# The second product of an MLP by Strassen's seven block products, with its sums on GpSimd

## The reference, cut to what matters

```python
D_MODEL, SEQ, D_FF = 1024, 512, 4 * 1024

def second_block(x, ...):
    ...
    h = rms_norm_2(x, norm_mlp[l])
    x = x + jnp.square(jax.nn.relu(h @ w_up[l])) @ w_down[l]
    return rms_norm_2(x, norm_final)
```

## Time and profile before

| | before |
|---|---|
| median of 3 runs | 1278.03 us (1277.8 to 1279.31) |
| the profiled execution: time | 1278.07 us |
| the profiled execution: span of the core | 1276.3 us |
| PE busy | 1226.8 us of the span (96%) |
| DVE, ACT, POOL busy | 669.9, 554.9, 119.0 us |
| mean granted TensorE clock | 0.989 of full speed |

### The profile page before, as it was taken

One profiled execution on the slowest core, in us unless ns is written; L12 is line 12 of the kernel. 1 busy time (PEld: TensorE's weight loads), 2 busy tenths in 40 slices (PEclk: granted clock), 3 DMA queues, 4 the chain that ended last, 5 costly groups with the idle time before them and its releaser, 6 DMA issues.

```text
span 1276.3 us, 16512 instructions
## 1 busy us (share of the span) xinstructions
PE 1226.8 (96%) x6162; PEld 1018.2 (80%) x6162; DVE 669.9 (52%) x1039; ACT 554.9 (43%) x952; POOL 119.0 (9%) x193
## 2 busy tenths in 40 slices
PE   7999999989999989999989899989999999999996
PEld 5877887768888788887778798877898888888885
DVE  5556567855333365683476665445553343443443
ACT  4456686674233245533665454342342241331321
POOL 2023223200000011000132000010000000000000
PEclk9999999999999999999999999999999999999998
DMA  5321233112333533342120455311323233323221
GB/s 169 99 67 50 69 87 110 34 51 68 98 99 108 188 117 117 83 140 76 33 108 25 149 140 172 118 50 40 94 87 111 84 99 99 99 99 99 84 97 66
DMA packets 148226, 120.64 MB, mean 95 GB/s; under 512 B 4865, under 2 KB 123713, under 8 KB 148162
## 3 DMA queue, kind: packets, MB, share of 16 engines
q1 hardware_dynamic: 142672, 106.05, 28.1%
q10 hardware_dynamic: 5490, 13.73, 3.1%
HBM read 115.55 MB, written 4.22 MB: 94 GB/s over the span
## 4 chain that ended last, share of the span: by engine, by line
PE 87%; DVE 6%; ACT 3%; DMA 2%; issue 1%; POOL 0%; ACTq 0%; DVEq 0%; SPq 0%
PE lin L748 26%; PE lin L750 25%; PE lin L749 25%; PE tr L906 2%; DVE w_lo L1877 2%; DMA x_m<-in_x 1%; PE sc L916 1%; PE sc L918 1%; PE tr L899 1%; ACT w_hi L1257 1%; PE lin L942 1%; DVE neg_max L1902 1%; DMA w_raw<-in_w_xkv 1%; PE lin L941 1%; DVE h_lo L1872 1%
## 5 line engine op out<-in xcount | busy, mean ns | idle before, releaser
L1877 DVE TENSOR_TENSOR w_lo<-w_raw,w_hi 128x1024 fp32r<-128x1024 f32 x194 | 237.5, 1229 | 236.7 <-ACT w_hi L1257 226.2
L748 PE MATMUL lin<-h_hi,w_hi 128*128 128x512 f32 (+1 forms) x848 | 326.2, 385 | 5.0 <-DVE h_lo L1872 4.6
L750 PE MATMUL lin<-h_hi,w_lo 128*128 128x512 f32 (+1 forms) x848 | 318.2, 375 | 0.0
L749 PE MATMUL lin<-h_lo,w_hi 128*128 128x512 f32 (+1 forms) x848 | 317.9, 375 | 0.0
L1257 ACT ACTIVATE w_hi<-w_raw 128x1024 fp32r<-128x1024 f32 x194 | 204.0, 1055 | 240.2 <-PE lin L750 164.9
L748 PEld LDWEIGHTS lin<-h_hi,w_hi 128*128 128x128 f32 x848 | 160.9, 190 | 34.2 <-DVE h_lo L1872 5.3
L750 PEld LDWEIGHTS lin<-h_hi,w_lo 128*128 128x128 f32 x848 | 160.6, 189 | 29.0
L749 PEld LDWEIGHTS lin<-h_lo,w_hi 128*128 128x128 f32 x848 | 161.1, 190 | 25.3 <-issue 0.2
L748 PE MATMUL lin<-w_hi,u_hi 128*128 128x512 f32 x256 | 99.6, 389 | 0.0
L749 PE MATMUL lin<-w_lo,u_hi 128*128 128x512 f32 x256 | 99.6, 389 | 0.0
L750 PE MATMUL lin<-w_hi,u_lo 128*128 128x512 f32 x256 | 99.6, 389 | 0.0
(11 more groups left out here) (318 smaller groups left out, 1915.6 us busy)
## 6 DMA issues: line engine op xcount, KB each, us to landing
w_raw<-in_w_in SPq DMA_DIRECT2D x74, 512.0 KB, 3.9
w_raw<-in_w_up SPq DMA_DIRECT2D x32, 512.0 KB, 4.0
w_raw<-in_w_down SPq DMA_DIRECT2D x32, 512.0 KB, 3.6
w_raw<-in_w_out SPq DMA_DIRECT2D x16, 512.0 KB, 3.6
w_raw<-in_w_xkv SPq DMA_DIRECT2D x16, 512.0 KB, 4.3
w_raw<-in_w_branch SPq DMA_DIRECT2D x8, 512.0 KB, 3.8
w_raw<-in_w_xq SPq DMA_DIRECT2D x8, 512.0 KB, 3.7
w_raw<-in_w_xo SPq DMA_DIRECT2D x8, 512.0 KB, 3.7
```

The lines of the kernel that those rows point to most:

```text
L748: pe.matmul(o, lh, rh, start=start, stop=False)
L749: pe.matmul(o, lh, rl, start=False, stop=False)
L750: return pe.matmul(o, ll, rh, start=False, stop=stop)
L1877: return dve.tensor_tensor(out, x, as_f32(hi), ALU.subtract)
```

## The change

The chunk's down product is taken as a product of 2 x 2 blocks: u has blocks of 256 tokens x 512 hidden, `w_down`'s chunk blocks of 512 hidden x 512 columns. Instead of the 8 block products there are 7 (`DOWN`), each of 2 token tiles x 4 x 3 = 24 matmuls, on sums and differences of blocks.

- **Weights**: the four blocks of `w_down` are loaded into eight buffers `wd_a`, `wd_b` of 128 x 1024. POOL forms four sums or differences of them, each in two parts, in place (`weights_sum`, 8 instructions of 128 x 1024). ACT and DVE split the seven operands, 14 halves, into the same four slots (`down_hi`, `down_lo`).
- **Tokens**: u is kept unsplit in `u_raw`; POOL forms four sums of its blocks (`u_sum`, 4 instructions of 128 x 1024), and ACT and DVE split these too (`u_sum_hi`, `u_sum_lo`).
- **Results**: the seven products lie in the PSUM banks `sc`, `tr` and `lin`. ACT copies the first to `u2`; DVE adds products from PSUM to `x_res`, `u2` and `u3` (`add_down`, 14 instructions of 128 x 512 in place of 8), and POOL adds `u2` and `u3` to `x_res` (`add_partial`, 4 instructions of 128 x 1024).
- **Written out**: the chunks are no loop on any engine. SP's loads of `w_down` stand between those of `w_up`.
- **The end**: the square sums are taken in halves of a row, and the tiles are stored in the order 2, 3, 0, 1 (`FINAL_ORDER`).

```diff
+A11, A12, A22, S1, S2, S3, S4 = range(7)
+B11, B12, B21, B22 = range(4)
+DOWN = [Product("z", A11, 4, B11), Product("q", S3, 7, B12), Product("r", A12, 9, B21), Product("z", S2, 10, B11),
+        Product("v", A22, 9, B21), Product("z", S1, 11, B11), Product("q", S4, 12, B22)]
...
 @block.gpsimd
+            for it in range(FF_CHUNKS):
...
+                weights_sum(it, 0, B12, B22, B12, ALU.subtract)
+                pool.wait_ge(u_lo_s, UP_SPLITS * it + 4)
+                u_sum(it, 0, (0, 0), (0, 0), (1, 0), ALU.subtract)
+                split_done(pool, down_half(it, 0, 1))
+                weights_sum(it, 1, B11, B12, B11, ALU.add)
+                pool.wait_ge(u_lo_s, UP_SPLITS * it + 9)
+                u_sum(it, 1, (1, 0), (1, 0), (1, 1), ALU.add)
+                u_sum(it, 2, (1, 1), (1, 1), (0, 0), ALU.subtract)
+                pool.wait_ge(m1_copied, 2 * it + 2)
+                add_partial(it, 0, 0, 0, "u2")
+                split_done(pool, down_half(it, 2, 1))
+                weights_sum(it, 2, B21, B21, B11, ALU.subtract)
+                u_sum(it, 3, (0, 1), (0, 1), (1, 1), ALU.subtract)
+                split_done(pool, down_half(it, 3, 1))
+                weights_sum(it, 3, B11, B22, B11, ALU.subtract)
+                pool.wait_ge(down_read, 14 * it + 6)
+                add_partial(it, 1, 1, 0, "u3")
+                add_partial(it, 2, 1, 1, "u3")
+                pool.wait_ge(down_read, 14 * it + 12)
+                add_partial(it, 3, 0, 1, "u2")
...
 @block.tensor
+                for n, product in enumerate(DOWN):
+                    pe.wait_ge(u_lo_s, UP_SPLITS * it + product.splits)
...
+                    elif n == 5:
+                        pe.wait_ge(down_read, 14 * it + 4)
...
+                        for part in range(2):
+                            split_done(pe, down_half(it, n, part))
+                            for tile in range(2):
+                                mm = part_of_tile(part, tile)
...
 @block.vector
-                    for t in range(NT):
-                        add_to_x(G["mlp"][8 + 4 * j + t], t, j, off)
...
+                for k in range(OPS):
+                    if k == 5:
+                        dve.wait_ge(x_added, 4 * it + 1)
+                        add_down(it, 2, of_x(0, 0), of_x(0, 0))
+                    elif k == 7:
+                        add_down(it, 3, partial("u2"), partial("u2"))
+                        add_down(it, 1, partial("u3"), partial("u2"), 3)
+                    elif k == 9:
+                        dve.wait_ge(x_added, 4 * it + 2)
+                        add_down(it, 4, of_x(1, 0), of_x(1, 0))
+                    elif k == 11:
+                        dve.wait_ge(x_added, 4 * it + 3)
+                        add_down(it, 5, of_x(1, 1), of_x(1, 1))
+                        add_down(it, 5, partial("u2"), partial("u2"))
+                    elif k == 13:
+                        dve.wait_ge(x_added, 4 * it + 4)
+                        add_down(it, 6, of_x(0, 1), of_x(0, 1))
+                    behind_down_lo(it, k)
+                    if k == 2:
+                        u_sum_lo(it, 10, S2, (1, 1))
+                    elif k == 4:
+                        u_sum_lo(it, 11, S1, (1, 0))
+                    elif k == 6:
+                        u_sum_lo(it, 12, S4, (0, 1))
```

More of the change, by code:

```diff
@@ L111, in m_by_tiles, with seven_products @@
         self.half(name, 2)
+    def seven_products(self, name):
+        for n in range(len(DOWN)):
+            if n < len(DOWN) - 1:
+                for _ in range(2):
+                    self.steps += 1
+                    self.half(name, raw=False)
+            else:
+                self.steps += 2
+                self.half(name, 2, raw=False)
     def m_products(self, name, kind, n=1):
@@ L224, in make_plan @@
         p.t_halves("mlp", "AD", 8)
-        p.m_quarters("mlp", "D", 2)
+        p.seven_products("down")
     return p
@@ L470, in two_blocks_kernel @@
         u_lo_s = sem("u_lo_s")
+        wd_loaded = [sem(f"wd_loaded{i}") for i in range(8)]
+        t_made = sem("t_made")
+        s_made = sem("s_made")
+        m1_copied = sem("m1_copied")
+        down_read = sem("down_read")
+        x_added = sem("x_added")
         final_ready = sem("final_ready")
@@ L534, in raw_ready @@
         def raw_ready(engine, u, off=None):
-            engine.wait_ge(w_loaded[u % 2], 16 * (u // 2 + 1) + (off or HERE).half * 8)
+            r = RAW[u]
+            engine.wait_ge(w_loaded[r % 2], 16 * (r // 2 + 1) + (off or HERE).half * 8)
         def split_done(engine, u, off=HERE):
@@ L1818, in _, with down_hi @@
[L1818 to L1823, removed]
+            def down_hi(it, k):
+                n, part = divmod(k, 2)
+                u, place = down_half(it, n, part), DOWN[n].place
+                if n in (0, 2, 6):
+                    act.wait_ge(wd_loaded[2 * place + part], 16 * (it + 1))
+                else:
+                    act.wait_ge(t_made, 8 * it + 2 * {1: 0, 3: 1, 4: 2, 5: 3}[n] + part + 1)
+                slot_free(act, u)
+                act.activation(w_hi[u % SLOTS][:, :], wd(place, part), ACT.Copy).then_inc(w_hi_s, 1)
@@ new lines, in _, with final_square @@
+            squares = [0]
+            def final_square(tile, half):
+                x = B["x_res"][:, tile, T * half:T * half + T]
+                squares[0] += 1
+                square_sum(Q0["final"] + squares[0] - 1, N0["final"] + FINAL_ORDER.index(tile), x, B["junk3"][:, :], half)
+            act.wait_ge(lin_step, ST[G["mlp"][8 * FF_CHUNKS - 1]])
+            load(B["gain3"][:, :], row("norm_final_2"), gain_in[5])
+            last = 14 * (FF_CHUNKS - 1)
+            for tile, half, read in ((0, 0, 1), (1, 0, 2), (2, 0, 7), (3, 0, 8), (2, 1, 9), (3, 1, 10), (0, 1, 13),
+                                     (1, 1, 14)):
+                act.wait_ge(down_read, last + read)
+                final_square(tile, half)
@@ L2499, in _, with down_lo @@
[L2499 to L2505, removed]
-                if n >= 1:
[L2507 to L2511, removed]
+            def down_lo(it, k):
+                n, part = divmod(k, 2)
+                u = down_half(it, n, part)
+                dve.wait_ge(w_hi_s, u + 1)
+                lo_part(w_lo[u % SLOTS][:, :], wd(DOWN[n].place, part), w_hi[u % SLOTS][:, :]).then_inc(w_lo_s, 1)
@@ new lines, in partial, with add_down @@
+            def partial(name):
+                return lambda tile: B[name][:, tile, :]
+            def add_down(it, n, out, x, read=0):
+                for tile in range(2):
+                    dve.wait_ge(lin_step, down_step(it, n, tile if n == len(DOWN) - 1 else 1))
+                    if read:
+                        dve.wait_ge(down_read, 14 * it + read + tile)
+                    dve.tensor_tensor(out(tile), x(tile), down_bank(DOWN[n].banks, tile), ALU.add)                        .then_inc(down_read, 1)
```

257 lines of the change are left out of this document (190 added, 67 removed).

## The result

| | before | changed |
|---|---|---|
| median (4 runs each) | 1277.91 us (1276.72 to 1279.31) | 1296.65 us (1295.21 to 1298.17) |
| profiled execution: time, span | 1278.07, 1276.3 us | 1296.46, 1294.6 us |

The ratio is 1.0146, with a 95% interval of 1.0129 to 1.0164: the changed kernel is slower by 18.7 us, against 19 forecast.

What follows compares the result with a forecast made beforehand. In the MLP the number of matmuls on PE was taken to set the time. With DVE and POOL taking turns, 1278.07 + 16.5 (four chunks) + 2.3 (end) = 1296.9, say 1297 us; range 1264 to 1306, 8 in 10.

Steps and rivals of the forecast that it cites:

- Matmuls: PE in the MLP: seven products of 24 matmuls instead of eight, 5.44 us less per chunk, 21.8 us in all.
- Turns: DVE's splits and POOL's sums exclude each other for whole instructions, a sum holding 2.33 us and a split 1.07.
- The rival of sums that don't hold DVE: POOL's sums never make DVE wait, PE runs without a gap, 81.6 us a chunk, 1257 us; chance 0.16.
- The sum on POOL: One POOL sum of 1024 columns takes 2.45 us, with bounds of 2.0 and 2.59.
- The chunk: One MLP chunk takes 91.2 us instead of 87.1: 5.44 us saved, 9.6 us of waits.
- the timetable: Down phase from product 0's first matmul, instructions starting when engine, waits and turn allow: 47.7 us instead of 43.5.
- last up group split: DVE has split the last up group 2.5 us into the down phase; POOL may then continue its token sums.
- half 9 split: Ready at 30.8 us, after eight POOL sums and nine DVE splits; PE wants it at 24.5, 6.4 us late.
- half 13 split: Ready at 43.6 us, after POOL's second add; PE does three quarters of product 6 after it.
- The sign that I gave: PE idle for 9 to 10 us per chunk, nearly all in products 3 to 6, ended by DVE's splits.
- All four chunks: The longer chunks of the MLP, four together, cost +16.5 us.
- The end: After PE's last matmul: +1.3 us for DVE's last two adds, +1.0 for variances and scalings, 2.3 in all.

Runs made afterwards that it cites:

- e3: Changed kernel with POOL's sums cut to one column each, all waits and other instructions kept: 1255.28 us, ratio to the kernel before 0.9833.
- e5: Changed kernel with each POOL sum issued as two instructions of 512 columns: 1298.13 us, ratio to the kernel before 1.0171.
- e4: Changed kernel with POOL's sums cut to one column and three fills of 512 columns ahead of each: 1255.68 us, ratio to the kernel before 0.9832.
- e6: Kernel before with 64 thrown-away sums of 128 x 1024 added on POOL, 16 per MLP chunk, nothing waiting for them: 1287.2 us, ratio 1.0074.
- e9: Kernel before with thrown-away POOL sums in chunks 2 to 4 alone, 48 in all: 1276.35 us, ratio 0.9996.
- e2: Changed kernel with the eight weight sums of a chunk on DVE, token sums and adds to x_res still on POOL: 1290.46 us, ratio 1.0104.
- e10: Changed kernel with weight and token sums on DVE, only the four adds to x_res on POOL: 1277.35 us, ratio to the kernel before 0.9997.
- e1: Changed kernel with all sixteen sums of a chunk made by DVE instead of POOL: 1262.12 us, ratio to the kernel before 0.9886.

## Why the prediction was right

*Matmuls: right.* e3 shows it clean: 81.6 us a chunk, 22 us less in all.

*Turns: right.* A sum on POOL and a split on DVE exclude each other for whole instructions: 3.33 us per pair (forecast 3.4), records of 2.3 us when the sum is halved (e5), no waiting with fills that read nothing (e4, where 120 of the 192 fills ran beside a split). The rival of sums that don't hold DVE, 1257 us, is what e3 and e4 reach with nothing to hold it. The Trainium skill ("SBUF — State Buffer", section "Who interferes with whom") has this rule. The traces of e4 (splits of at most 1227 ns beside fills) and e5 (records that fall from 3.4 to 2.3 us with half sums) agree with it.

*The sum on POOL: 2.45 forecast, 2.38 to 2.41 measured*, its hold 2.26 in place of 2.33. The estimate by the Trainium skill ("GPSIMD Engine Reference", section "Performance versus the Vector engine"), 2.25 us, was 0.13 to 0.16 low.

*The chunk: 91.2 forecast, 91.3 measured, and step by step as in the timetable.* Counted from product 0's first matmul (1143.79 in the third chunk), in us:

| | forecast | third chunk |
|---|---|---|
| last up group split | 2.5 | 2.9 |
| half 9 split | 30.8 | 31.0 |
| half 11 split | 36.8 | 36.8 |
| half 12 split | 40.2 | 40.1 |
| half 13 split | 43.6 | 43.5 |
| down phase ends | 47.7 | 47.8 |

The start 0.4 us later and the eight sums 0.07 us shorter each partly cancel. The sign that I gave, PE idle for 9 to 10 us, was missed all the same, since PE spends its lateness in two ways. From start to start, less the 0.227 that is due, the five waits of the third chunk are 1.43, 0.49, 0.56, 3.70 and 1.33 us, 7.5 in all; the other 2.2 are matmuls that start late behind a wait, 1.6 of it at half the clock. In the second chunk the waits are 6.3 us, with 0.14 for half 13, and late matmuls 3.4, of which 2.8 at half the clock. The phase takes 47.79 us in both. DVE works without a pause from the split of half 3 until past half 13, so it is DVE and POOL that set when half 13 is there, and a slower PE only waits less for it. The clock is therefore not a term of its own here, though no run held it fixed.

*All four chunks: 16.5 forecast, 19.4 measured* (from the first matmul of the MLP to the last, 912.12 to 1282.63, against 914.76 to 1265.82). The first chunk is the mis-sized term: its down phase takes 50.2 us where the second and third take 47.8 (38.1 without waits), so it lost 12 us and they 9.7. DVE ended the last split of its up groups 5.3 us into that phase (964.09 - 958.76), against 2.9 in the third chunk, and this is the difference. e6 and e9 found the same in the kernel before: DVE enters the first chunk with a backlog. I had read DVE's slack in the third chunk and taken it for all four.

*The end: 2.3 forecast, 1.5 measured* (11.97 us from the last matmul's start to the end of the span, 10.48 before). The changed kernel's profiled execution also came to the MLP 2.6 us earlier; 19.4 + 1.5 - 2.6 is the 18.3 between the spans. The kernels of the experiments differ there by as much, with the same instructions, so it is no effect of the change. That the total came within 0.3 us of the 19 forecast is therefore in part luck: MLP and end cost 20.9 us, 2.1 more than forecast, and in the profiled execution the earlier start hid it.

*Open:* which engine has the next turn. POOL's add of `u3` had it after one split in the changed kernel and after two in e2 and e10, with the same 0.22 us between the starts, and no run shows why. e2's 7 us over my timetable are explained by it in part only (1.1 us of 1.75 per chunk).

## What to carry to other kernels

Before elementwise work is moved from DVE to POOL, look at where its operands lie: with two SBUF inputs on DVE and SBUF inputs on POOL, a sum of 1024 columns that was moved here spared DVE 1.14 us and could shut it out for 2.26. Work on two engines that exclude each other is to be added up as if it were one engine's, and best given to the faster; e1 does so, and turns 1.5% lost into 1.1% won. Read slack in every stage where the cost will fall, the first pass of a loop above all, and not in the steady one alone.

## What the runs showed of the hardware

- In the changed kernel PE, idle for 3.54 to 3.56 us, came back at a granted clock of 0.50 (1.2 GHz), its matmuls 0.43 us apart: eight in the third chunk, 14 in the second. Behind waits of 1.44 us and less it stayed at 1.00. In e10 a wait of 2.16 us was followed by 0.50 in the first chunk, and the same wait in the other chunks was not.
- Those slower matmuls cost nothing in the sum: the down phase took 47.79 us with 1.6 us lost to the clock and with 2.8, since half 13 came from DVE at 43.5 us in both.
- A turn is not strictly alternate: POOL's add took 3.25 us with one split ahead of it and 4.4 with two.
- Fills on POOL (526 ns for 128x512, 192 of them) leave DVE's splits at 1222 ns.
